# An MLA head's row maximum taken in two halves of 512 keys in an encoder block kernel

## What is computed

```python
def attend(qb):                                     # qb: one block of 128 queries
    s = jnp.einsum('bqhd,bshd->bhqs', qb, k) * scale    # 128 queries x 1040 keys a head
    p = jax.nn.softmax(s, axis=-1)                      # exp(s - max(s)) / sum
    return jnp.einsum('bhqs,bshd->bqhd', p, v)
```

## Time and profile before

| | |
|---|---|
| three runs | 2378.54, 2379.91, 2384.56 us; median 2379.91 us |
| profiled execution | 2364.12 us; its span 2362.4 us |
| TensorE (PE) busy | 2254.7 us, 95% |
| weight loads (PEld) busy | 1696.0 us, 72% |
| VectorE (DVE) busy | 779.7 us, 33% |
| ScalarE (ACT) busy | 459.1 us, 19% |
| mean granted TensorE clock | 0.983 of full speed |

### The profile page before, as it was taken

One profiled execution on the slowest core, in us unless ns is written; L12 is line 12 of the kernel. 1 busy time (PEld: TensorE's weight loads), 2 busy tenths in 40 slices (PEclk: granted clock), 3 DMA queues, 4 the chain that ended last, 5 costly groups with the idle time before them and its releaser, 6 DMA issues.

```text
span 2362.4 us, 36881 instructions
## 1 busy us (share of the span) xinstructions
PE 2254.7 (95%) x15236; PEld 1696.0 (72%) x15236; DVE 779.7 (33%) x2243; ACT 459.1 (19%) x1148; POOL 216.3 (9%) x248
## 2 busy tenths in 40 slices
PE   6999899999999679999999999999999999999997
PEld 3555466666666477777888878887887887878875
DVE  3554544445444322222222222222222222222221
ACT  2333434444344200000100001000100000000000
POOL 0000000000000211111211112110000100000000
PEclk9999999999999789999999999999999999999998
DMA  4000500000000199787788888998999899899881
GB/s 156 18 11 1 163 10 28 28 19 10 28 28 28 37 355 334 257 286 267 258 305 302 305 303 270 315 320 316 320 329 340 307 338 345 308 336 332 308 297 19
DMA packets 212009, 492.25 MB, mean 208 GB/s; under 512 B 24608, under 2 KB 28480, under 8 KB 211664
## 3 DMA queue, kind: packets, MB, share of 16 engines
q1 hardware_dynamic: 192112, 449.79, 52.1%
q0 software_dynamic: 16080, 38.27, 6.9%
q10 hardware_dynamic: 3648, 1.79, 0.3%
HBM read 464.59 MB, written 29.82 MB: 209 GB/s over the span
## 4 chain that ended last, share of the span: by engine, by line
PE 64%; DMA 0%; issue 0%; POOL 0%; ACT 0%; POOLq 0%; DVE 0%; ACTq 0%
PE gu_bank L1690 41%; PE ya_bank L1704 19%; PE yb_bank L1717 3%; PE xa_bank L1660 1%; PE xb_bank L1668 0%; DMA tab_b<-slot_table 0%; DMA x_rows<-ffn_rows,tab 0%; POOL out_y L1433 0%; ACT y_rows L1503 0%; POOL slot_table L552 0%; POOLq L1413 0%; DVE y_rows L1566 0%; POOL tab_b L1397 0%; ACTq L1520 0%; PE yb_bank L1731 0%
## 5 line engine op out<-in xcount | busy, mean ns | idle before, releaser
L1690 PEld LDWEIGHTS gu_bank<-xT,ring 128*128 128x128 f32 x8192 | 964.1, 192 | 14.7 <-issue 14.6
L1690 PE MATMUL gu_bank<-xT,ring 128*128 128x128 f32 (+10 forms) x8192 | 968.0, 281 | 0.8 <-issue 0.8
L1704 PE MATMUL ya_bank<-ring,hidden 128*128 128x512 f32 x1024 | 446.2, 594 | 0.0
L1704 PEld LDWEIGHTS ya_bank<-ring,hidden 128*128 128x128 f32 x1024 | 192.4, 190 | 229.6 <-issue 225.2
L1543 DVE TENSOR_SCALAR g_in<-gu_bank,bias_cur 128x128 f32<-128x128 f32 (+10 forms) x256 | 92.1, 360 | 684.3 <-PE gu_bank L1690 684.3
L1497 ACT ACTIVATE sig<-g_in 128x128 f32<-128x128 f32 (+10 forms) x256 | 81.0, 317 | 882.7 <-DVE g_in L1543 882.7
L1566 DVE TENSOR_TENSOR y_rows<-ya_bank,b_row 128x512 f32<-128x512 f32 x64 | 41.3, 686 | 380.1 <-PE ya_bank L1704 380.1
L485 PE MATMUL proj_bank<-w_in_sb,normT 128*128 128x512 f32 (+3 forms) x432 | 149.6, 501 | 13.7 <-DVE w_in_sb L370 12.9
L1433 POOL DMA_INDIRECT out_y<-y_rows,tab x32 | 51.8, 1620 | 960.8 <-ACT y_rows L1503 960.8
L1503 ACT ACTIVATE y_rows<-y_rows,tab 128x512 f32<-128x512 f32 x64 | 42.7, 714 | 478.2 <-DVE y_rows L1566 478.2
L485 PEld LDWEIGHTS proj_bank<-w_in_sb,normT 128*128 128x128 f32 (+1 forms) x432 | 70.9, 182 | 82.2 <-issue 78.8
(11 more groups left out here) (243 smaller groups left out, 1723.0 us busy)
## 6 DMA issues: line engine op xcount, KB each, us to landing
ring<-in_w_gate SPq DMA_DIRECT2D x64, 2048.0 KB, 13.0
ring<-in_w_up SPq DMA_DIRECT2D x64, 2048.0 KB, 11.2
ring<-in_w_down SPq DMA_DIRECT2D x64, 2048.0 KB, 13.7
b_row<-in_b_down SPq DMA_DIRECT2D x32, 512.0 KB, 10.2
w_in_sb<-in_w_in SPq DMA_DIRECT2D x8, 592.0 KB, 9.0
xt<-in_x SPq DMA_DIRECT2D x8, 512.0 KB, 4.0
resid<-in_x SPq DMA_DIRECT2D x8, 512.0 KB, 4.3
out_y<-resid SPq DMA_DIRECT2D x8, 512.0 KB, 2.6
```

Source lines behind the costliest of these rows:

```text
L1690: last = nc.tensor.matmul(gu_bank[:, f % 2, i * 256:i * 256 + width], w[:, k, c * P:(c + 1) * P], xT[:, k, 0:width], start=(k == 0), stop= ...
L1704: last = nc.tensor.matmul(ya_bank[:, h, :], hidden[:, k, 0:P], w[:, k % 4, h * 512:(h + 1) * 512], start=(k == 0), stop=(k == FC - 1))
```

## The change

The maximum of an MLA head's 1024 scores is taken by two reductions of 512 and a maximum of the two results. TensorE increments a new semaphore, `half_done`, on the matmul that finishes keys 0 to 511; VectorE waits for it and reduces the first half, then waits for `scores_done` as before, reduces the second half, waits for its own result, joins the two (`all_max`), waits again, and goes on with L946. `real_max` grows from one number to two for each of its two buffers. Nothing else is moved.

```diff
-        real_max = m.sb("real_max", [P, 2])
+        real_max = m.sb("real_max", [P, 2, 2])
+        all_max = m.sb("all_max", [P, 2])
...
+        half_done = m.sem("half_done")
...
                         j = at_fill["unit", n]
+                        if i < MLA_HEADS:
+                            dve.wait_ge(half_done, t * MLA_HEADS + i + 1)
+                            v.tensor_reduce(real_max[:, n % 2, 0:1], score_bank[:, j % 2, 0:512], AX.X, ALU.max)
                         dve.wait_ge(scores_done, j + 1)
                         if i < MLA_HEADS:
 
                             if i == 0:
                                 dve.wait_ge(meta_read, t + 1)
-                            link(v.tensor_reduce(real_max[:, n % 2:n % 2 + 1], score_bank[:, j % 2, :], AX.X, ALU.max))
+                            link(v.tensor_reduce(real_max[:, n % 2, 1:2], score_bank[:, j % 2, 512:1024], AX.X, ALU.max))
+                            link(v.tensor_tensor(all_max[:, n % 2:n % 2 + 1], real_max[:, n % 2, 0:1],
+                                                 real_max[:, n % 2, 1:2], ALU.max))
                             if n >= 2:
                                 dve.wait_ge(exp_done, n - 1)
-                            v.tensor_scalar(neg_max[:, n % 2:n % 2 + 1], real_max[:, n % 2:n % 2 + 1],
+                            v.tensor_scalar(neg_max[:, n % 2:n % 2 + 1], all_max[:, n % 2:n % 2 + 1],
                                             meta_max[:, t % 2, i:i + 1], -1.0, ALU.max, ALU.mult).then_inc(max_ready, 1)
...
                             last = nc.tensor.matmul(bank[:, half * 512:(half + 1) * 512], mla_qT[:, i, cols(t)],
                                                     mla_kT[:, i, half * 512:(half + 1) * 512], start=True, stop=True)
+                            if half == 0:
+                                last.then_inc(half_done, 1)
```

## The result

Five runs of the changed kernel gave 2360.94 to 2370.25 us, median 2365.60; five of the kernel before 2377.99 to 2384.56, median 2379.91. The ratio is 0.9937 (95% interval 0.9917 to 0.9957): **faster by 0.6%, about 14 us**.

What follows compares the result with a forecast made beforehand. TensorE was taken to bound attention and experts, so only its waits for the maximum counted: 5.1 + 1.75 + 0.6 = 7.5 us, from 2379.91 to 2372.4 us. The range was 2366 to 2382.

Steps and rivals of the forecast that it cites:

- The chain: From the end of the scores through maximum, negation and exponentials to TensorE's transposes: 0.35 us shorter, 0.19 to 0.37.
- The covers: Costs priced at nothing: head 3's later maximum, hidden by the output projection (else 2.4 us), and TensorE's 64 extra increments.
- the slower rival: The increment breaks TensorE's score stream: 14.9 us slower, 2394.8; chance 0.09 together with any other loss.
- What the waits give back: TensorE's waits in attention shrink: exponentials 5.1, router's matmuls 1.75, router's transposes 0.6, 7.5 us in all.
- the router's transposes: Six TensorE waits of 0.35 us behind head 4's maximum: cut by 0.1 each, 0.6 us.
- The router's matmuls: Five TensorE waits of about 0.76 us behind head 6's maximum: cut by 0.35 each, 1.75 us.
- head 7: Four waits of its transposes for the exponentials: 0.32 us lost at each, all of it to go.
- head 2: Seven waits for exponentials of 0.56 us each, ahead of TensorE's transposes: cut by the full 0.35.
- the offset of the median: The runs' median lay 15.8 us above the profiled execution; taken to stay, as nothing in the stage touched explains it.
- The clock rival: Clock drops in attention tiles vanish: gain 11.8 us, 2368, chance 0.12; or more drops: 2375 to 2381, chance 0.12.
- The checks promised: Profile signs: negation 0.95 us after the scores, transposes' waits 7.3 to about 3, router's matmuls about 2, score groups unstretched.
- The full-clock tile of 66.5 us: Profile sign: an attention tile at full clock takes 66.5 to 66.6 us instead of 67.72.

Runs made afterwards that it cites:

- the second profiles: Profiled executions from running both kernels once more without edits: 2387.81 us for the kernel before, 2369.36 us for the changed kernel.
- before again: The kernel before, run and profiled once more with no edit: 2380.16 us over 12 runs, ratio 1.0001.
- after again: The changed kernel, run and profiled once more with no edit: 2365.47 us, ratio 0.9939 against the kernel before.
- the padded kernel: The changed kernel with three extra overwritten matmuls ahead of head 1's scores in every tile: 2376.02 us, 0.9984 against the kernel before.
- the runs of before sorted by clock: No new kernel: 76 runs of the unchanged kernel grouped by mean clock; medians from 2383.88 us at 0.976 to 2374.32 us at 0.980 to 0.981.
- late halves: Against the kernel before: two reductions and the join, both only after all scores are done, without the half_done increment: 2393.88 us, ratio 1.0056.
- increment alone: The kernel before plus TensorE's half_done increment and VectorE's wait for it, still one reduction of 1024: 2386.55 us, ratio 1.0025.
- the first half alone: The changed kernel without the second reduction and join, maximum of keys 0 to 511 only: 2367.29 us, 0.9952 against the kernel before.
- after with the meta scores first: The changed kernel with VectorE reading the meta scores ahead of head 6's maximum: 2364.44 us, 0.9943 against the kernel before.

## Why the prediction was wrong by half, point by point

**The chain: right.** 0.34 us shorter (1.30 to 0.96) where 0.35 was worked out; reduction, join, start before the end of the scores and VectorE's load came within 0.01 us or 2%.

**The covers: right.** Head 3's first half begins only at 451.35, with no idle time ahead of it, and nobody waits for the result: behind it stands the output projection. The increment does not stretch TensorE's score groups, so the slower rival is dead. The Trainium skill ("TensorE: Matmul & The Clock Gate", The cost: per-tile semaphore tail) prices a serialised increment at 26.3 ns, 1.7 us by that estimate for 64; score groups of 1.98 and 1.88 us with and without it show none of that.

**What the waits give back: right, but summed too low.** 13.2 to 3.8 us is 9.4 (between the second profiles, 12.0 to 3.8, it is 8.2), where 7.5 was summed. The mis-sized term is the router's transposes, 0.1 us each. The starts within one tile at full clock, before again against after again, counted from the output projection, show 17.97 to 17.71 there: 0.26 us, because VectorE starts instructions back to back sooner than their durations say: there the residual addition (1.22 us), the first and the second reduction start at 468.03, 469.17 and 469.77 in after. The router's matmuls gave another 0.34 (0.35 taken), head 7 0.32 (0.32) and head 2 0.33 (0.35). One tile: 1.26 us where 1.12 was summed.

**The clock, carried along in the offset of the median: the step that failed.** "Nothing in the stage touched explains that offset, and I take it to stay." With this the sum put the falls of the clock at nothing. The second profile of before showed that 19.8 of 23.7 us of such an offset lie in that very stage. Some 10 us are the six scatter stalls, which the change leaves as they are; these stay, as assumed. The rest is falls of the clock, and here the change does act. Between the two kernels, tiles 2 to 6 took 354.8 us in before again and 340.1 in after: 14.7 us, of which 6.3 are waits (5 x 1.26) and 7.7 the falls (6.3 and 1.4) that before again had there and after had not. That pair of executions is an extreme one; over all runs the clock's share is 14.3 - 9.4 = 5 us by difference, about 3 us by the padded kernel and an estimated 5 us by the runs of before sorted by clock. So of the 6.8 us that the forecast missed, some 2 are waits summed too low and some 5 the clock.

**The clock rival was named and given too little weight.** Its 7.5 + 4.3 = 11.8 us came nearest, and that the result missed the range by only 0.4 us is owed to this rival, which had set its lower end. It was given 4.3 us and a chance of 0.12, from an execution with a clock of 0.983 that had two falls in tiles 2 to 6; runs of before have 0.978. Its argument, "there are five such waits and two falls, so the wait is no sufficient cause", was true and the wrong one to lean on: the late halves had longer waits and a fall in each of five tiles. How long the waits are against how much the kernel gained or lost:

| kernel | sum of the three waits, us | gained against before, us | clock |
|---|---|---|---|
| late halves | 17.5 | -13.4 | 0.975 |
| increment alone | 13.0 | -6 | 0.976 |
| before again | 12.0 | 0 | 0.978 |
| after again | 3.8 | 14.5 | 0.981 |

Each step of this table moves the time by more than the waits. That the clock carries the excess fits the mean clocks and the places of the falls. It is not shown as a law, and why the clock falls less with the change stays open: the first half alone and after with the meta scores first have still shorter waits and gained nothing on after, and tile 1 had falls without a wait.

**The checks promised.** Those on the chain, on the waits (7.3 to 1.7; "about 3" was said) and on the score groups held. The full-clock tile of 66.5 us did not appear: 68.0 is 66.4 and the stall of 1.6.

## What to carry to other kernels

Before a small change is priced against "the profile", compare that execution's time and mean clock with those of the ordinary runs; here the only profile of before was 15.8 us quick. It lacked the scatter stalls, so that its tiles looked shorter than those after the change, and had a mean clock of 0.983 where the runs have 0.978. Splitting an operation into more, dearer pieces pays when its first piece runs in time that its engine idles away and another engine waits for its end (0.69 + 0.69 + 0.16 us in place of 1.23, and 0.6% gained); split without the early start, it lost as much. Where TensorE is busy 95% of the time, removing short waits may give one and a half to two times what the view of waits says (9.4 us of waits and 14.3 of time; 3.8 and 7), with a higher mean clock; it may also give nothing (the meta scores first on after, 2.1 us).

## What the runs showed of the hardware that was not expected

- **Scatters and TensorE.** Indirect DMAs issued by GpSimd beside unrelated work went with a stop of TensorE in mid-stream and a copy of ScalarE that came late, 1.64 us in each of six tiles; gone where they were left out or moved, and absent in one execution that had them.
- **The clock.** It fell to half speed behind waits of 0.3 to 1.0 us, with TensorE otherwise busy (1.01 us, then a granted clock of 0.54), and in tile 1 behind sixteen matmuls of 16 columns with no wait at all (0.50). Which wait or which small matmuls bring a fall, no run here tells.
- **VectorE.** Two reductions with no wait between them start 0.59 us apart (451.35 and 451.94) though each lasts 0.68. The prediction added them up. With a second semaphore wait ahead of it, long met, the maximum started 0.11 instead of 0.04 us after the scores.
